# Gated delta rule scan: the block inverse taken from its transpose by an identity product, and state products split around the right product

## The reference

```python
a_mat = jnp.where(strict, jnp.einsum('bhnid,bhnjd->bhnij', kb, k) * decay, 0.0)
t_mat = lax.linalg.triangular_solve(eye + a_mat, jnp.broadcast_to(eye, a_mat.shape),
                                    left_side=True, lower=True, unit_diagonal=True)
u = jnp.einsum('bhnij,bhnjd->bhnid', t_mat, vb)
w = jnp.einsum('bhnij,bhnjd->bhnid', t_mat, kb * jnp.exp(gc)[..., None])
...
def step(s, inp):
    u_i, w_i, qk_i, qd_i, kd_i, gl_i = inp
    v_new = u_i - jnp.einsum('bhcd,bhde->bhce', w_i, s)
    o_i = jnp.einsum('bhcd,bhde->bhce', qd_i, s) + jnp.einsum('bhcj,bhje->bhce', qk_i, v_new)
    s = s * gl_i[..., None, None] + jnp.einsum('bhcd,bhce->bhde', kd_i, v_new)
    return s, o_i
```

## Time and profile before

| | |
|---|---|
| median of 3 runs | 2855.58 us (2854.47 to 2855.85) |
| the profiled execution | 2855.78 us, span 2854.0 us |
| TensorE busy | 2598.5 us, 91% of the span |
| VectorE busy | 1660.1 us, 58% |
| ScalarE busy | 646.7 us, 23% |
| GpSimd busy | 1132.1 us, 40% |
| first scan | 1372 to 1549 us from the start of the span |
| second scan | 1680 to 1857 us |

### The profile page before, as it was taken

How to read it: one execution, slowest core, us unless ns; L and a number is a source line. 1 busy time by engine, 2 the same in 40 slices (tenths; PEclk the granted TensorE clock), 3 DMA queues, 4 the chain that set the end, 5 groups by cost and what they waited for, 6 DMA issues and landing times. The chain is left out here.

```text
span 2854.0 us, 45433 instructions
## 1 busy us (share of the span) xinstructions
PE 2598.5 (91%) x18610; PEld 2172.5 (76%) x18610; DVE 1660.1 (58%) x2509; ACT 646.7 (23%) x1253; POOL 1132.1 (40%) x922
## 2 busy tenths in 40 slices
PE   8989999989889999987699959977798999899998
PEld 6778888777578888776588848864587788688887
DVE  7858668473558758576555655533476615463351
ACT  4122012101322112233443244311254210110000
POOL 3545554453045555432321332211333444444553
PEclk9999999999999999998899979988999999999999
DMA  4224343321033343210011101011200222223232
GB/s 153 103 93 151 111 150 124 117 74 60 1 133 133 123 143 134 86 63 31 24 40 46 59 16 33 32 35 41 52 23 6 104 89 103 87 75 103 89 103 74
DMA packets 51316, 229.68 MB, mean 80 GB/s; under 512 B 5296, under 2 KB 12480, under 8 KB 32576
## 3 DMA queue, kind: packets, MB, share of 16 engines
q1 hardware_dynamic: 51136, 227.10, 23.2%
HBM read 224.91 MB, written 2.17 MB: 80 GB/s over the span
## 5 line engine op out<-in xcount | busy, mean ns | idle before, releaser
L246 POOL TENSOR_TENSOR ring_rounded<-ring,ring_rounded 128x512 fp32r<-128x512 f32 (+2 forms) x715 | 937.5, 1342 | 1152.6 <-DVE ring_rounded L237 1141.9
L286 PE MATMUL psum<-arena_rounded,ring_rounded 128*128 128x512 f32 (+1 forms) x2820 | 1098.8, 390 | 63.4 <-PEq L515 13.7
L287 PE MATMUL psum<-arena_rounded,ring_rounded 128*128 128x512 f32 (+1 forms) x2820 | 1090.9, 387 | 0.0
L288 PE MATMUL psum<-arena_rounded,ring_rounded 128*128 128x512 f32 (+1 forms) x2820 | 1089.6, 386 | 0.0
L286 PEld LDWEIGHTS psum<-arena_rounded,ring_rounded 128*128 128x128 f32 x2820 | 536.5, 190 | 185.9 <-issue 47.6
L288 PEld LDWEIGHTS psum<-arena_rounded,ring_rounded 128*128 128x128 f32 x2820 | 536.2, 190 | 107.7
L287 PEld LDWEIGHTS psum<-arena_rounded,ring_rounded 128*128 128x128 f32 x2820 | 536.8, 190 | 105.0 <-issue 1.5
L237 DVE CAST ring_rounded<-ring 128x2048 fp32r<-128x2048 f32 (+4 forms) x191 | 212.4, 1112 | 686.4 <-PE psum L288 625.0
L713 ACT ACTIVATE arena<-psum,vectors 128x512 f32<-128x512 f32 x88 | 68.6, 782 | 409.0 <-PE psum L288 409.0
L329 DVE TENSOR_TENSOR arena_rounded<-arena,arena_rounded 128x512 fp32r<-128x512 f32 (+2 forms) x113 | 125.3, 1108 | 3.9
L327 DVE CAST arena_rounded<-arena 128x512 fp32r<-128x512 f32 (+2 forms) x113 | 114.1, 1010 | 9.2 <-DVE arena L743 1.0
(11 more groups left out here) (394 smaller groups left out, 3054.3 us busy)
## 6 DMA issues: line engine op xcount, KB each, us to landing
ring<-in_w_up SPq DMA_DIRECT2D x44, 1024.0 KB, 4.8
arena<-in_w_mod SPq DMA_DIRECT2D x48, 512.0 KB, 3.4
ring<-in_w_down SPq DMA_DIRECT2D x32, 704.0 KB, 3.9
ring<-in_w_mup SPq DMA_DIRECT2D x16, 1024.0 KB, 4.8
ring<-in_w_mdown SPq DMA_DIRECT2D x16, 1024.0 KB, 4.8
ring<-in_w_gdn SPq DMA_DIRECT2D x12, 1024.0 KB, 4.9
ring<-in_w_lru_in SPq DMA_DIRECT2D x10, 1024.0 KB, 4.8
ring<-in_w_odd_in SPq DMA_DIRECT2D x10, 1024.0 KB, 4.8
```

The source lines that it names most:

```text
L246: last = pool.tensor_tensor(self.rounded(low), raw, self.rounded(high).bitcast(F32), ALU.subtract)
L286: pe.matmul(out, r(wh), r(xh), start=start, stop=False)
L287: pe.matmul(out, r(wh), r(xl), start=False, stop=False)
L288: return pe.matmul(out, r(wl), r(xh), start=False, stop=stop)
```

## The change

Z is no longer summed up by products of its own. After each level X is copied to SBUF as before, and a new step `turn` multiplies each block of X by the identity, which gives its transpose Z, in 16 products over the four quadrants. On TensorE turn(k-1) stands behind left(k), and the last one behind far_left. The seed no longer writes Z. ScalarE's copy of Z waits for the turn (`zturn`) instead of `zmul`; its place in ScalarE's list is the same. And the pieces of the recurrence are split by direction: direction 0 stands ahead of right(k), direction 1 behind it.

```diff
@@ seed
                 pe.wait_ge(sem("z1", d), count("z1", d, t + 1))
                 if t:
-                    pe.wait_ge(sem("zdiag", d), count("zdiag", d, t))
                     pe.wait_ge(sem("xcopy", d), count("xcopy", d, 6 * t))
...
-            for d in range(2):
-                for r in half:
-                    pe.matmul(m.psum[r, 4 * d + ZB, 0:GH * HB], m.ident[r, r],
-                              B[d]["Z1"][r].rearrange("p a b -> p (a b)"), start=True, stop=False, skip_group_check=True)
@@ right
                             last.then_inc(up("xmul", d), 1)
+
+        def turn(t, k):
             for d in range(2):
-                for h in range(GH):
-                    for r in half:
-                        last = pe.matmul(compact(d, ZB)[r, h, :], B[d]["YC"][r, h, :], z[d][r, h, :], start=False,
-                                         stop=False, skip_group_check=True)
-                last.then_inc(up("zmul", d), 1)
+                pe.wait_ge(sem("xcopy", d), count("xcopy", d, 6 * t + 1 + k))
+            for h in range(GH):
+                for i in range(2):
+                    for d in range(2):
+                        x, z = half[i], place(d, i)
+                        last = pe.matmul(compact(d, ZB)[z, h, :], B[d]["XC"][x, h, :], m.ident[x, x], start=True,
+                                         stop=True)
+                        if h == GH - 1 and i == 1:
+                            last.then_inc(up("zturn", d), 1)
@@ pe
+        def beside(t, k, d):
+            if k == 1 and t >= 2:
+                state_product(t - 1, d)
+            if k == 2 and 2 <= t + 1 < NA:
+                query_gram(t + 1, d)
+            if k == 3 and t + 1 < NA:
+                gram(t + 1, d)
+            if k == 4 and t:
+                inverse_product(t - 1, d)
+            if k == 5 and t:
+                state_update(t - 1, d)
+
...
             for k in range(1, LEVELS + 1):
                 left(t, k)
-                for d in range(2):
...
+                if k > 1:
+                    turn(t, k - 1)
+                beside(t, k, 0)
                 right(t, k)
+                beside(t, k, 1)
             far_left(t, 0)
             far_left(t, 1)
+            turn(t, LEVELS)
@@ act, z_copy
-            act.wait_ge(sem("zmul", d), count("zmul", d, LEVELS * t + k))
+            act.wait_ge(sem("zturn", d), count("zturn", d, LEVELS * t + k))
@@ dve, triangle
-                dve.wait_ge(sem("zmul", d), count("zmul", d, LEVELS * (t - 1) + 1))
+                dve.wait_ge(sem("xmul", d), count("xmul", d, 6 * (t - 1) + 2))
```

## The result

The changed kernel takes 2896.14 us (median of 4 runs, 2892.48 to 2898.03) against 2855.72 us for the kernel before: the ratio is 1.0141, 95% interval 1.0123 to 1.0158. That is 40 us slower. The forecast was 2875 us, its range ended at 2893: the sign was right, the size half of what came.

A forecast was written before the change was run, and what follows sets the result against it. In the two scans TensorE never rests over a middle tile's first two levels, with latency beneath; the first tile runs by latency. 8.2 us a scan, 16.4 in all, gave 2872.2, plus 2.6 for clock: 2875 us; 8-in-10 range 2857 to 2893.

The forecast's parts named there:

- Point 1: On TensorE, L2118 (1.03 us a level) goes; the turn replacing it issues in 0.52 us, 0.62 before a 128x128 product.
- Points 2 and 3: ScalarE: copy of Z starts 1.27 us after left(k+1), exponentials 1.81 us after left(2); left(2) to left(3) becomes 4.92 us.
- Point 4: Next tile's Gram: its first half starts 0.52 us later behind the turn, so triangles and right(4) come 0.52 us later.
- Point 5: Split pieces behind right(k): 0.99 us of product, 1.61 us to the next left; left(2) 3.3 us after left(1), before 4.16.
- Point 6: Last turn behind far_left: right(5) to output 2.75 us for 2.13; in first three tiles right(5) to seed 5.03 for 3.44.
- The clock, 2.6 us: TensorE's lower clock: one more slowed level a scan, 2 x 1.3 us, taking the forecast to 2875 us.
- rival C: Clock falls with the gaps: some 8 levels a scan at 1.2 GHz, +21 us on 2872, giving 2893 us; chance 0.15.
- the sum: Tile-by-tile total at full clock over both scans: 8.2 us a scan, 16.4 us in all, giving 2872.2 us.
- Rival A: TensorE bounds throughout: each of 60 levels gains 0.41 us, -25 us, 2831 us; chance 0.09.

The follow-up runs named there:

- e7_decay_parted: Changed kernel with direction 0's four exponentials ahead of level 1's copy of Z on ScalarE, direction 1's behind it: 2889.5 us, 1.0114 to the kernel before.
- e3_query_late: Changed kernel with GpSimd's product for the queries moved behind the next tile's first level: 2890.5 us, 1.0113 to the kernel before.
- e13_warm_all: Changed kernel with unread identity products in gaps of all six tiles, 36 ahead of the first seed: 2881.2 us, 1.0083 to the kernel before.
- e5b_warm_gaps: Changed kernel with unread identity products, 26 ahead of the first seed and 1 to 8 per gap in the first three tiles: 2885.4 us, 1.0100.
- e9_orders: Changed kernel with direction 0's exponentials earlier, second triangle behind level 4's masks, queries' product behind next tile's first level, last turn ahead of far_left: 2861.7 us.
- e10_orders_warm: e9_orders with unread identity products in gaps of early and last tiles, 36 ahead of the first seed: 2848.96 us, 0.9971 to the kernel before.

## Why the prediction was right or wrong

1. *Point 1, the turn issues in 0.52 us, or 0.62 ahead of a 128x128 product.* Right: the turn starts at 1509.92 and the 128x128 product behind it at 1510.50, 0.58 us later.
2. *Points 2 and 3, the copy of Z and the exponentials behind it.* Right: left(2) to left(3) 4.87 us for 4.92, and e7_decay_parted took half of the exponentials away from it and got 3.90.
3. *Point 4, right(4) +0.52 us.* Too small. I assumed that the 5.50 us from the triangle's start to right(4) would stay. It became 6.16 (1516.63 to 1522.79), since the triangle now starts together with GpSimd's product (1516.73) and its first pair takes 1.90 us where it took 1.25. Moving that product (e3_query_late) took 5.6 us off the kernel, part of it perhaps by the clock.
4. *Point 5.* Left(2) 3.43 us after left(1) for 3.3: half a piece between two groups of 64x64 issues in 1.09 us (1508.32 to 1509.41), not 0.99.
5. *Point 6, the tiles' ends.* A little small. In the fifth tile right(5) to the output is 3.07 us (1526.68 to 1529.75) for 2.75. In the third, right(5) to the next seed was 5.6 us (1467.14 to 1472.76) for 5.03, of which 0.55 us are a stall in the middle of right(5), for which the profile shows no releaser.
6. *The clock, 2.6 us.* This is the step that failed. I priced one slower level a scan, from the level behind the 2.15 us wait of the kernel before. In the changed kernel most of the first tile ran at 1.2 GHz in both scans (0.74 and 0.61), and so did parts of the second, third and sixth tile in the first scan and of the second and fourth in the other. The fillers of e13_warm_all brought 15 us back. So the clock is the larger part of the 21 us that the forecast lacked, though not all of it, and some of what the fillers mended was low clock that the kernel before had too. The clock was rival C, to which I gave 0.15 and whose 2893 us was near. I argued against it from one gap of 1.05 us in the kernel before that left the clock alone. But the first tile of the changed kernel has gaps of 0.84 to 1.72 us in each of its first three levels. Nor does a single gap tell the price the other way: the 2.08 us ahead of its right(4) left the clock up through level 5, and a wait of 2.36 us in the fifth tile did too, where one of 2.38 us in e7_decay_parted did not. The Trainium skill ("TensorE: Matmul & The Clock Gate", section "What's actually happening") calls the throttled clock the default, which activity releases. These runs agree: a group takes 1.13 us in the first levels of the first tile without fillers, and 0.69 us from its second level on with those of e5b_warm_gaps.
7. The remaining 9 us (2881 for 2872) are the misses of points 4 to 6 of the sum and what the fillers cost. The fifth tile, at 1.00 in both kernels, grew by 1.8 us for 0.7: 0.6 us too much at right(4), 0.3 at the end, 0.1 each at level 5 and over the first two levels. Stalls of TensorE for which the profile shows no releaser came to 0.3 us in the second scan before and to 2.0 us after (1.6 and 1.8 in the first scan); the sum had no term for them, why they grew is open, and no run shows that such stalls come from fetching instructions, as the sum said of one. How the 9 us divide over the kernel was not measured.

Rival A fell as argued: the decays decide. But it had a truth in it. With the orders of the other engines mended (e9_orders), a level does take 3.9 us instead of 4.16.

## What to carry to other kernels

When TensorE's list is made shorter, read what the other engines' lists have standing between the two copies that now limit it; each engine's order was fitted to the old one, and here the mending of the lists of ScalarE, VectorE and GpSimd, with the last turn put ahead of far_left, was worth 34 us, most of the loss. A change in two parts is not the sum of its parts: turn and split cost 2.7 us each in a tile, together 1.8, and with the right order less than nothing. Do not price the clock by what one gap of the old schedule did: gaps of nearly the same length left it up in one place and brought it down in another. Where a new schedule puts short rests into every level, give the lower clock a range of its own, and measure it with fillers, in both kernels: what they give to the old one is not the change's.

## What the runs showed of the hardware

- Products that nothing reads, put into gaps of 0.8 to 2.4 us, shorten three tiles by 1.8 to 3.3 us each (e5b_warm_gaps); 26 ahead of the first seed left a rest of 3.19 us and the seed still ran at 1.13 us a group, 36 left 0.72 us and it ran at 0.69 (e13_warm_all; 1.75 us and 0.69 in e10_orders_warm).
- VectorE's product of two SBUF operands (64x256, two of them) takes 0.85 us alone (e3_query_late) and 1.90 us beside GpSimd's product of two SBUF operands (1.25 where that had started 1.95 us earlier and not 1.07); its instructions that read PSUM beside it kept their 1.13 us.
